# Two-block transformer kernel: the second layer's slabs in another order, the last up slab in narrow matmuls, and moved steps on four engines

## The chip, the cores and the metric

The kernel runs on one core of a Trainium2 chip. The metric is the device time of one execution in microseconds (us), lower is better. Engines: TensorE (PE) multiplies, ScalarE (ACT), VectorE (DVE) and GpSimd (POOL) do the rest, SyncE (SP) issues the loads. They run side by side and wait for each other on semaphores; each works through its own queue in order.

## What is computed

Two blocks, one after the other, on 256 tokens of width 1024, all in float32. The first is a mixer (8 heads of softmax attention, 4 heads of gated linear attention) and an FFN with a three-tap convolution over the tokens; then a norm with a gain; the second is a mixer of four branches and an FFN. Cut to what matters here:

```python
# first block, after its mixer
hn = rms_norm(x, ffn_norm_g[l])
h = causal_dwconv(hn @ w_ffn_up[l], conv_w[l], conv_b[l])     # 3 taps + bias
h_gate, h_val = h[..., :D_FF], h[..., D_FF:]                  # D_FF = 2816
x = x + (jax.nn.silu(h_gate) * h_val) @ w_ffn_down[l]
...
return rms_norm(x, final_norm_g)
# second block, mixer
proj = xn @ w_in
(cb, cc, cx, uv, sb_q, sb_k, sb_v, fx_q, fx_k, fx_v, f_raw, gate_raw) = split(proj)
y_a = cb * conv(cc * cx)                         # short convolution
y_b = u * (tril(w_s) @ layer_norm(v) + b_s)      # u, v = gelu(uv): spatial gate
y_c = stick_breaking_attention(sb_q, sb_k, sb_v)             # 4 heads of 64
log_f = log_sigmoid(f_raw + b_f)
y_d = forgetting_attention(rms(fx_q), rms(fx_k), fx_v, cumsum(log_f))   # 4 heads of 64
merged = sum over n of sigmoid(gate_n) * (y_n @ w_branch_n)
h = h + merged @ w_out
```

## The kernel before

**Slabs.** All weights are cut into 117 slabs of 1 MB (`STREAM`), each [128, 8, 256] for a projection of 256 columns. `AT` gives a slab's number n. A slab is loaded by SyncE into `raw` (3 buffers), rounded by ScalarE to a high part `hiw` (`rnd`, L611), and VectorE forms the rest `low = raw - hiw` (`res`, L1054), 3 buffers each. Activations are kept as a high and a low part as well (`xhi`, `xlo`; `yhi`, `ylo`), and a product is three matmuls: high by high, low by high, high by low (`three`, L1709 to L1711). `rnd(n)` waits until TensorE has used slab n-3 (`consumed`), `res(n)` for `rnd(n)`, and TensorE for `hi_made` and `lo_made` of its slab.

**Orders.** The order of the work is written out by hand on each engine: PE, ACT and DVE each have a loop over k, the slab's place in the stage (`for k, name in enumerate(IN2 + EARLY)` on PE, `for k in range(19)` on the others), in which `if k == ...` places the small steps of attention and convolution. A step that waits holds everything behind it on its engine.

**PSUM** has 8 banks of [128, 512]. `tenant(name, bank)` lists who uses a bank in which order; `take_bank` waits until the tenant before has given it back, `frees` gives it back.

**End of the first mixer.** `out_1(c)` runs the four slabs of the output projection in the order o0, o2, o3, o1; each is four quarters of six matmuls (`out_slab`, `out_quarter`). Between them TensorE turns the probabilities of heads 6 and 7 (`turn_probs`, L1894) and multiplies them with the values (`moba_values(3)`, called in slab o3 after its first quarter). ScalarE makes the high part of the two gated pairs (`gla_hi`, L757), VectorE the low part (`gla_lo`, L1273).

**First FFN.** For each of 11 steps f: slabs g_f and v_f (up), d_f (down). An up slab is `feature_major_wide` (L1733, L1741): 16 matmuls of 512 columns take `xhi` and `xlo` side by side and leave two partial sums, and 16 of 256 add the low part of the weights. VectorE adds the two sums (`hidden_sum`, L1324) into SBUF, ScalarE applies the last tap and the bias (`tap2s`, L858), VectorE the other two taps (`conv`, L1342), ScalarE the silu of the gate half, VectorE the product (`gate_1`, L1354), ScalarE its high part (`y_high`, L875), VectorE its low part (`y_low`, L1369). `last_two` writes out steps 9 and 10. TensorE ends with `ffn_down_last_two`: tile 0 (tokens 0 to 127) of d9 and d10, then tile 1.

**The norm between the blocks** (`weighted_norm` on DVE). As soon as a quarter is done, VectorE adds it to `h` (`quarter`, L1085), ScalarE squares it, VectorE sums the squares with weights (`weighted_sum`, L1108), GpSimd takes the root (L539), and the rows are scaled, one half by VectorE (`rows`, L1115), one by ScalarE (L652). TensorE turns a tile by 8 transposes (`turn_tile`, L1666), ScalarE writes `xhi` (`tile_turned`, L661), VectorE `xlo` (L1125).

**Second layer.** `IN2` is sq, sk, sv, fq, fk, fv, cc, cx, cb, u, v. The first slab (sq) is computed tile by tile, token-major (`tile_slab`, L1681, L1682, L1689), written out by ScalarE (`rows_out`, L668) and turned back by four transposes (`turn_back`, L1698) inside sv. sk uses `feature_major_late` (L1764, L1769), the others `project`. Steps in between: `stick_scores` (L2058, L2060), `stick_sums` (L2068), `fox_norm`, the product for the forget gates (`small_product("f")`), `fox_scores`, `turn_probs`.

## Time and profile before

| | us |
|---|---|
| median of 3 runs | 734.34 |
| runs | 734.33 to 734.43 |
| profiled execution | 734.29 |
| its span, first to last instruction | 732.5 |
| TensorE busy | 719.8 |
| VectorE busy | 546.8 |
| ScalarE busy | 379.8 |
| GpSimd busy | 56.9 |

The difference of 1.8 us between execution and span is what lies around the instructions. Stages on the trace's clock: first mixer to 131, first FFN to 321, second mixer to 543, second FFN to the end. A row of the timeline gives start, duration, engine, line, operation, names and shapes, count, and in brackets the idle time before it with what ended it. Matmuls are pipelined, so the duration of one is longer than the distance to the next start.

### The profile page before, as it was taken

The page shows a single profiled execution, that of the slowest core. Times are in us where ns is not written, and L with a number is a line of the kernel's source. Part 1 is how long each engine was busy: PE and PEld are TensorE (multiplying, and loading weights), DVE is VectorE, ACT ScalarE, POOL GpSimd, SP SyncE. Part 2 cuts the span into 40 slices and gives each one's busy share as a digit, 9 for nine tenths or more (in the row PEclk, how much of TensorE's full clock was granted, in tenths as well). Part 3 has the DMA queues.
Part 4 walks back from the last instruction along what each step waited for, and adds up shares of the span by engine and source line. Part 5 has one row for each costly group of instructions (what it writes and reads, how often), then busy time and mean ns, then how long its engine had stood idle before and what let it go on. Part 6 is the DMA issues. An engine that isn't in the chain of part 4 may idle for free.

```text
span 732.5 us, 11499 instructions
## 1 busy us (share of the span) xinstructions
PE 719.8 (98%) x4488; PEld 637.4 (87%) x4488; DVE 546.8 (75%) x645; ACT 379.8 (52%) x471; POOL 56.9 (8%) x62
## 2 busy tenths in 40 slices
PE   8999999999999999989999999999999999999998
PEld 8999987888888888778999888989888888888886
DVE  6679937889998889966557858787788666656673
ACT  7635466666455455556564544544456344343341
POOL 1455100000330000011000000000000000000000
PEclk9999999999999999999999999999999999999999
DMA  9846334255555455324543444445435554455431
GB/s 363 319 134 201 117 115 162 81 218 222 180 205 196 172 190 212 119 111 154 197 163 129 164 173 173 173 173 222 180 115 201 205 200 198 172 199 202 174 115 57
DMA packets 18954, 129.27 MB, mean 176 GB/s; under 512 B 2272, under 2 KB 2528, under 8 KB 3680
## 3 DMA queue, kind: packets, MB, share of 16 engines
q1 hardware_dynamic: 18912, 128.68, 47.4%
q8 instruction: 30, 0.49, 0.3%
q14 instruction: 12, 0.10, 0.0%
HBM read 126.57 MB, written 1.05 MB: 174 GB/s over the span
## 4 chain that ended last, share of the span: by engine, by line
PE 92%; DVE 3%; ACT 2%; issue 1%; DMA 1%; POOL 0%; SPq 0%; DVEq 0%; ACTq 0%
PE ps L1733 20%; PE ps L1709 14%; PE ps L1710 13%; PE ps L1711 13%; PE ps L1741 10%; PE ps L1753 8%; PE ps L1755 4%; DVE low L1054 1%; PE ps L1871 1%; ACT hiw L611 1%; PE ps L1681 1%; PE ps L1689 1%; PE ps L1682 1%; PE ps L1666 1%; DMA h<-in_x 1%
## 5 line engine op out<-in xcount | busy, mean ns | idle before, releaser
L611 ACT ACTIVATE hiw<-raw 128x2048 fp32r<-128x2048 f32 x116 | 222.0, 1915 | 203.6 <-PE ps L1741 97.7
L1054 DVE TENSOR_TENSOR low<-raw,hiw 128x2048 fp32r<-128x2048 f32 x116 | 267.2, 2308 | 79.4 <-ACT hiw L611 78.7
L1733 PE MATMUL ps<-xx,hiw 128*128 128x512 f32 x672 | 159.9, 390 | 0.0
L1733 PEld LDWEIGHTS ps<-xx,hiw 128*128 128x128 f32 x672 | 124.5, 188 | 24.8
L1741 PEld LDWEIGHTS ps<-xx,low 128*128 128x128 f32 x672 | 86.0, 191 | 3.1
L1741 PE MATMUL ps<-xx,low 128*128 128x256 f32 x672 | 87.3, 283 | 0.0
L1709 PE MATMUL ps<-hiw,yhi 128*128 128x512 f32 x208 | 81.8, 393 | 1.6 <-DVE ylo L1369 1.5
L1710 PE MATMUL ps<-low,yhi 128*128 128x512 f32 x208 | 81.2, 390 | 0.0
L1711 PE MATMUL ps<-hiw,ylo 128*128 128x512 f32 x208 | 80.9, 389 | 0.0
L1324 DVE TENSOR_REDUCE arena<-ps 128x512 f32<-128x1024 f32 x42 | 51.3, 1221 | 24.1 <-PE ps L1741 24.0
L1709 PE MATMUL ps<-xx,hiw 128*128 128x256 f32 x224 | 64.3, 287 | 1.0 <-DVE low L1054 1.0
L1753 PE MATMUL ps<-xx,hiw 128*128 128x512 f32 x256 | 64.7, 394 | 0.0
L1710 PE MATMUL ps<-xx,hiw 128*128 128x256 f32 x224 | 63.4, 283 | 0.0
L1711 PE MATMUL ps<-xx,low 128*128 128x256 f32 x224 | 63.3, 283 | 0.0
L1753 PEld LDWEIGHTS ps<-xx,hiw 128*128 128x128 f32 x256 | 46.1, 189 | 8.9 <-issue 0.5
L1709 PEld LDWEIGHTS ps<-hiw,yhi 128*128 128x128 f32 x208 | 39.1, 188 | 10.1 <-DVE ylo L1369 1.9
L1711 PEld LDWEIGHTS ps<-hiw,ylo 128*128 128x128 f32 x208 | 39.0, 188 | 8.3
L1710 PEld LDWEIGHTS ps<-low,yhi 128*128 128x128 f32 x208 | 39.1, 188 | 7.2
L1342 DVE SCALAR_TENSOR_TENSOR arena<-arena,vec 128x255 f32<-128x255 f32 x88 | 40.5, 481 | 5.8 <-ACT arena L858 1.5
L1709 PEld LDWEIGHTS ps<-xx,hiw 128*128 128x128 f32 x224 | 42.9, 192 | 2.0 <-issue 1.7
L1710 PEld LDWEIGHTS ps<-xx,hiw 128*128 128x128 f32 x224 | 42.9, 192 | 0.0
L1711 PEld LDWEIGHTS ps<-xx,low 128*128 128x128 f32 x224 | 42.9, 192 | 0.0
(240 smaller groups left out, 1022.2 us busy)
## 6 DMA issues: line engine op xcount, KB each, us to landing
raw<-in_slabs SPq DMA_DIRECT2D x117, 1024.0 KB, 4.8
vec<-in_vec SPq DMA_DIRECT2D x1, 1258.5 KB, 9.2
cst<-in_cst SPq DMA_DIRECT2D x1, 1220.0 KB, 12.8
h<-in_x SPq DMA_DIRECT2D x2, 512.0 KB, 3.6
arena<-arena SPq DMA_DIRECT2D x16, 64.0 KB, 2.9
out<-h SPq DMA_DIRECT2D x1, 512.0 KB, 2.7
out<-h SPq DMA_DIRECT2D x2, 256.0 KB, 2.0
vec<-in_vec SPq DMA_DIRECT2D x1, 229.0 KB, 4.3
```

What stands on the lines that cost most here:

```text
L611: act.activation(hiw[:, n % SPLIT, :], raw[:, n % RAW, :], ACT.Copy).then_inc(hi_made, 1)
L1054: dve.tensor_tensor(low[:, n % SPLIT, :], raw[:, n % RAW, :], hiw[:, n % SPLIT, :].bitcast(F32), ALU.subtract).then_inc(lo_made, 1)
L1324: dve.tensor_reduce((hid if k == "ffn1" else up)[par][j], wide_hidden(j).rearrange("p c (a b) -> p c b a", a=2), AX_X, ALU.add).then_inc(h ...
L1342: ins = dve.scalar_tensor_tensor(out=dst[:, o:], in0=src[:, 0:T - o], scalar=w, in1=dst[:, o:], op0=ALU.mult, op1=ALU.add)
L1666: mm = pe.transpose(bank(name)[:, k * P:(k + 1) * P], hn[n][:, tt, kt * P:(kt + 1) * P], ident)
L1709: pe.matmul(o, whi, mhi, start=start, stop=False)
L1710: pe.matmul(o, whi, mlo, start=False, stop=False)
L1711: return pe.matmul(o, wlo, mhi, start=False, stop=stop)
L1733: pe.matmul(banks[:, c, :], hi[:, kt, cc_], xx[:, kt].rearrange("p a b -> p (a b)"), start=kt == 0, stop=False)
L1741: mm = pe.matmul(banks[:, c, 0:T], lo[:, kt, cc_], xhi[:, kt, :], start=False, stop=kt == KT - 1)
L1753: pe.matmul(o, hi[:, kt, cc_], xx[:, kt].rearrange("p a b -> p (a b)"), start=kt == 0, stop=False)
L1755: mm = pe.matmul(o[:, 0:T], lo[:, kt, cc_], xhi[:, kt, :], start=False, stop=kt == KT - 1)
```

## The change

1. **Second layer.** `IN2` becomes v, sv, sq, sk, fq, fk, fv, cc, cx, cb, u. The first two are computed by the new `value_tile`, tile by tile and in parts ("both" = xhi by high and low weights, "high", "low", "second" = xlo by high weights), and stay token-major. `tile_slab`, `rows_out` and `turn_back` are no longer used there. Banks are dealt out anew, and the steps placed by k move: stick attention two slabs later, fox attention one, convolution one, the layer norm and the spatial gate one. The product for the forget gates goes from k = 7 to k = 3, its bias to k = 4, its exponential and logarithm to k = 6 and the forget sums from k = 8 to k = 7.
2. **Last up slab** (v10 of the first FFN): 48 matmuls of 256 columns into two banks (`last_up`) in place of the wide form; ScalarE (`last_tap2s`) and VectorE (`last_conv`) read PSUM directly, and `hidden_sum` falls away for it.
3. **Norm between the blocks.** VectorE scales both halves of tile 0's rows (`late_rows`), ahead of the third quarter. Tile 1's weighted sums stand after all low halves of tile 0, ScalarE rounds sv ahead of tile 0's high halves, and VectorE takes sv's residual (`res(second)`) ahead of tile 1's low halves.
4. **End of the first mixer.** Head 7 is turned inside slab o3, after its first quarter, its values follow after the second. The high part of the first gated pair is a copy on VectorE.

```diff
-IN2 = ["sq", "sk", "sv", "fq", "fk", "fv", "cc", "cx", "cb", "u", "v"]
+IN2 = ["v", "sv", "sq", "sk", "fq", "fk", "fv", "cc", "cx", "cb", "u"]
...
+        for n, b in (("v", 0), ("sv", 1), ("sq", 2), ("sk", 3), ("fq", 6), ("fk", 7), ("fv", 0), ("cc", 1), ("cx", 0),
+                     ("cb", 1), ("u", 0)):
...
+        tenant("f", 4)
...
-            for j in range(2):
-                gla_hi(j)
+            gla_hi(1)
...
+            def last_tap2s():
+
+                act.wait_ge(*hidden_full("ffn1", FF - 1, 1))
+                for c in range(2):
+                    ch = NCH // 2 + 2 * (FF - 1) + c
+                    act.activation(yb[0][:, 2 + c, :], last_hidden(c), ACT.Identity,
+                                   scale=V("cw")[:, 2 * NCH + ch:2 * NCH + ch + 1],
+                                   bias=V("cb")[:, ch:ch + 1]).then_inc(s("tap2"), 1)
...
                 tap2s(g, 0)
                 rnd(before[2][0])
                 silu_1(g)
+                last_tap2s()
                 rnd(after[2][0])
-                tap2s(g, 1)
                 y_high("ffn1", g)
                 rnd(after[3][0])
...
             for nh in range(2):
                 square(2, 0, nh)
-            rows(2, 0)
-            square(2, 1, 0)
+            rnd(b2 + 1)
             tile_turned(2, 0)
-            square(2, 1, 1)
-            rnd(b2 + 1)
+            for nh in range(2):
+                square(2, 1, nh)
             rows(2, 1)
             tile_turned(2, 1)
-            for tt in range(TT):
-                rows_out(2, 0, tt)
             rnd(b2 + 2)
...
-                if k == 7:
+                    forget_gates()
+                if k in (7, 9):
...
+            def late_rows(n, tt):
+
+                dve.wait_ge(s("root_made"), 2 * (n - 1) + tt + 1)
+                dve.tensor_scalar(hn[n][:, tt, D // 2:], h[:, tt, D // 2:], norm_scale(n, tt), None,
+                                  ALU.mult).then_inc(s("rows_b"), 1)
...
-            def weighted_norm(used):
+            def weighted_norm(used, second):
 
                 quarter(2, 0, used)
                 quarter(2, 1, used)
                 for nh in range(2):
                     weighted_sum(0, nh)
+                rows(2, 0)
+                late_rows(2, 0)
                 quarter(2, 2, used)
-                rows(2, 0)
-                weighted_sum(1, 0)
                 tile_turned(2, 0, range(0, 4))
                 quarter(2, 3, used)
-                tile_turned(2, 0, range(4, 6))
-                weighted_sum(1, 1)
-                tile_turned(2, 0, range(6, 8))
+                tile_turned(2, 0, range(4, 8))
+                for nh in range(2):
+                    weighted_sum(1, nh)
                 rows(2, 1)
+                res(second)
                 tile_turned(2, 1, range(8))
...
-            gla_norm(0)
-            gla_scaled(1)
+            for j in range(2):
+                gla_scaled(j)
+            gla_gated(0)
+            dve.wait_ge(s("gy_made"), 1)
+            dve.tensor_copy(yhi[:, 4:6, :], orr[0]).then_inc(s("gy_hi"), 1)
             gla_lo(0)
             gla_gated(1)
...
+            def last_conv():
+
+                f = FF - 1
+                for c in range(2):
+                    ch = NCH // 2 + 2 * f + c
+                    dve.wait_ge(s("tap2"), 4 * f + 2 + c + 1)
+                    dst, src = yb[0][:, 2 + c, :], last_hidden(c)
+                    for tap in (1, 0):
+                        o = 2 - tap
+                        ins = dve.scalar_tensor_tensor(out=dst[:, o:], in0=src[:, 0:T - o],
+                                                       scalar=V("cw")[:, tap * NCH + ch:tap * NCH + ch + 1],
+                                                       in1=dst[:, o:], op0=ALU.mult, op1=ALU.add)
+                        if tap:
+                            me.step(dve, ins)
+                        else:
+                            ins.then_inc(s("conv_made"), 1)
...
                 y_low("ffn1", f)
                 conv(g, 0)
                 split_all(before[2])
-                hidden_sum("ffn1", g, 1)
-                conv(g, 1)
+                last_conv()
...
-                if k == 6:
+                if k == 8:
                     for j in range(2):
                         fox_normed(j)
-                if 2 <= k <= 5:
-                    stick_soft(k - 2)
-                if k in (5, 7):
-                    head_lo(f"so{(k - 5) // 2}", 4 + (k - 5) // 2)
-                if k == 8:
+                if 4 <= k <= 7:
+                    stick_soft(k - 4)
+                if k in (7, 9):
+                    head_lo(f"so{(k - 7) // 2}", 4 + (k - 7) // 2)
+                if k == 7:
+                    forget_sums()
+                if k == 9:
...
                         mm = pe.matmul(o[:, 0:T], lo[:, kt, cc_], xhi[:, kt, :], start=False, stop=kt == KT - 1)
                     mm.then_inc(*fills(f"{name}_{c}"))
 
+            def value_tile(name, tt, parts, last=True):
+
+                n = AT[("in2", name)]
+                hi, lo = slab_views(n, KT)
+                t_ = slice(tt * P, (tt + 1) * P)
+                o = bank(name)[:, tt * 256:(tt + 1) * 256]
+                mm = None
+                for part in parts:
+                    if part == "high":
+                        pe.wait_ge(hi_made, n + 1)
+                    elif part in ("both", "low"):
+                        pe.wait_ge(lo_made, n + 1)
+                    for kt in range(KT):
+                        stop = last and part == parts[-1] and kt == KT - 1
+                        if part in ("high", "both"):
+                            if kt % 2 == 0:
+                                pe.wait_ge(s("xhi_made"), KT + 16 + 8 * tt + kt + 2)
+                            mm = pe.matmul(o, xhi[:, kt, t_], hi[:, kt, :], start=kt == 0, stop=False)
+                        if part in ("low", "both"):
+                            mm = pe.matmul(o, xhi[:, kt, t_], lo[:, kt, :], start=False, stop=stop)
+                        if part == "second":
+                            if kt % 2 == 0:
+                                turned, k = turned_at(2, tt, kt)
+                                pe.wait_ge(*part_given(turned, k + 2))
+                            mm = pe.matmul(o, xlo[:, kt, t_], hi[:, kt, :], start=False, stop=stop)
+                return mm
+
             def feature_major_late(o, n):
...
-                    if q == 1 and middle is not None:
-                        middle()
+                    if q in (1, 2) and middle is not None:
+                        middle[q - 1]()
                     mm = out_quarter(n, q, chunks, yh, yl, accs[q], first, last)
...
-            turn_probs(7, "mt7", pex1)
-            out_1(2, lambda: moba_values(3))
+            out_1(2, (lambda: turn_probs(7, "mt7", pex1), lambda: moba_values(3)))
             out_1(3)
...
+            def last_up():
+
+                n = AT[("ffn1", f"v{FF - 1}")]
+                pe.wait_ge(*hidden_free("ffn1", FF - 1, 1, done=False))
+                pe.wait_ge(lo_made, n + 1)
+                hi, lo = slab_views(n, KT)
+                for c in range(2):
+                    cc_ = slice(c * P, (c + 1) * P)
+                    for kt in range(KT):
+                        mm = three(last_hidden(c), hi[:, kt, cc_], lo[:, kt, cc_], xhi[:, kt, :], xlo[:, kt, :], kt == 0,
+                                   kt == KT - 1)
+                mm.then_inc(hidden_full("ffn1", FF - 1, 1)[0], 1)
...
-                ffn_up(k, FF - 1)
+                if k == "ffn1":
+                    ffn_up(k, FF - 1, parts=1)
+                    last_up()
+                else:
+                    ffn_up(k, FF - 1)
...
             for k, name in enumerate(IN2 + EARLY):
-                how = token_major if name in ("sv", "fv", "v") else feature_major
+                how = token_major if name == "fv" else feature_major
                 if k == 0:
-                    tile_slab(2, 0, 0)
+                    take_bank(pe, "v")
+                    value_tile("v", 0, ("both", "second"))
+                    take_bank(pe, "sv")
+                    value_tile("sv", 0, ("high", "second"), False)
                     turn_tile(2, 1)
-                    tile_slab(2, 0, 1)
+                    value_tile("v", 1, ("both",), False)
+                    value_tile("sv", 0, ("low",))
+                    value_tile("v", 1, ("second",)).then_inc(*fills("v"))
                 elif k == 1:
-                    take_bank(pe, name)
-                    pe.wait_ge(hi_made, AT[("in2", name)] + 1)
-                    feature_major_late(bank(name), AT[("in2", name)]).then_inc(*fills(name))
-                elif k == 2:
-                    def back():
-                        take_bank(pe, "sq")
-                        turn_back(2, 0, bank("sq")).then_inc(*fills("sq"))
-
-                    project("in2", name, lambda o, n: token_major(o, n, back))
+                    value_tile("sv", 1, ("both", "second")).then_inc(*fills("sv"))
                 elif name in EARLY:
                     gate_slab("in2", name)
                 else:
                     project("in2", name, how)
...
+                if k == 3:
+                    small_product("f", slice(16, 144))
+                if k == 8:
                     for j in range(2):
                         fox_norm(j)
```

**TensorE, from the turning of tile 0 to the turning of tile 1.** `tile_slab` for sq is L1681, L1682 (products) and L1689; in the change `value_tile` is L1812 (high weights), L1814 (low weights) and L1819 (xlo). Before:

```order
L1711 MATMUL ps<-hiw,ylo 128x512
L1666 MATMUL ps<-cst,arena 128x128 x8
L1709 MATMUL ps<-hiw,yhi 128x512
L1710 MATMUL ps<-low,yhi 128x512
...
L1711 MATMUL ps<-hiw,ylo 128x512
L1681 MATMUL ps<-hiw,xx 128x256
L1682 MATMUL ps<-low,xx 128x256
...
L1689 MATMUL ps<-hiw,xx 128x256 x8
L1666 MATMUL ps<-cst,arena 128x128 x8
```

Now:

```order
L1748 MATMUL ps<-hiw,ylo 128x512
L1703 MATMUL ps<-cst,arena 128x128 x8
L1746 MATMUL ps<-hiw,yhi 128x512
L1747 MATMUL ps<-low,yhi 128x512
...
L1748 MATMUL ps<-hiw,ylo 128x512
L1812 MATMUL ps<-hiw,xx 128x256
L1814 MATMUL ps<-low,xx 128x256
...
L1819 MATMUL ps<-hiw,xx 128x256 x8
L1812 MATMUL ps<-hiw,xx 128x256 x8
L1819 MATMUL ps<-hiw,xx 128x256 x8
L1703 MATMUL ps<-cst,arena 128x128 x8
```

Between the two turnings (L1666, now L1703) stood the last quarter and one tile of sq; now the last quarter, tile 0 of v, and 16 matmuls of tile 0 of sv stand there.

**VectorE, from the last up slab to the turning of tile 0.** L1324 is the sum of the partials, L1342 and L1377 the taps, L1054 and L1067 residuals, L1085 and L1098 the additions to `h`, L1115, L1128 and L1134 the scaled rows. Before:

```order
L1054 TENSOR_TENSOR low<-raw,hiw 128x2048
L1324 TENSOR_REDUCE arena<-ps 128x512
L1342 SCALAR_TENSOR_TENSOR arena<-arena,vec 128x255
...
L1354 TENSOR_TENSOR arena<-arena 128x512
L1054 TENSOR_TENSOR low<-raw,hiw 128x2048
L1369 TENSOR_TENSOR ylo<-arena,yhi 128x512
L1054 TENSOR_TENSOR low<-raw,hiw 128x2048
L1085 TENSOR_TENSOR h<-ps,h 128x512 x2
L1108 ISA arena,st<-arena 128x512
...
L1085 TENSOR_TENSOR h<-ps,h 128x512
L1115 TENSOR_SCALAR arena<-h,st 128x512
```

Now:

```order
L1067 TENSOR_TENSOR low<-raw,hiw 128x2048
L1377 SCALAR_TENSOR_TENSOR arena<-ps,vec,arena 128x255
L1377 SCALAR_TENSOR_TENSOR arena<-ps,vec,arena 128x254
...
L1391 TENSOR_TENSOR arena<-arena 128x512
L1067 TENSOR_TENSOR low<-raw,hiw 128x2048
L1406 TENSOR_TENSOR ylo<-arena,yhi 128x512
L1067 TENSOR_TENSOR low<-raw,hiw 128x2048
L1098 TENSOR_TENSOR h<-ps,h 128x512 x2
...
L1128 TENSOR_SCALAR arena<-h,st 128x512
L1134 TENSOR_SCALAR arena<-h,st 128x512
L1098 TENSOR_TENSOR h<-ps,h 128x512
```

The sum is gone, the taps read PSUM, and the rows come in two halves ahead of the third quarter's addition.

**VectorE, at the forget sums.** L1484 to L1490 (now L1520 to L1526) are the forget sums, L1469 (now L1504) the stick argument, L1478 (now L1513) the fox query and key. Before, at k = 8:

```order
L1501 SCALAR_TENSOR_TENSOR arena<-arena,vec 128x255
L1501 SCALAR_TENSOR_TENSOR arena<-arena,vec 128x254
L1565 TENSOR_TENSOR arena<-ps,arena 128x512
L1484 SCALAR_TENSOR_TENSOR arena<-arena 128x256
L1486 SCALAR_TENSOR_TENSOR arena<-arena 128x256
L1490 TENSOR_SCALAR arena<-arena 2x2x256 x4
L1054 TENSOR_TENSOR low<-raw,hiw 128x2048
L1444 TENSOR_TENSOR ylo<-arena,yhi 128x512
```

Now, at k = 7 and 8:

```order
L1067 TENSOR_TENSOR low<-raw,hiw 128x2048
L1498 SCALAR_TENSOR_TENSOR arena<-arena 128x384
L1269 TENSOR_TENSOR ylo<-ps,yhi 128x256
L1520 SCALAR_TENSOR_TENSOR arena<-arena 128x256
L1522 SCALAR_TENSOR_TENSOR arena<-arena 128x256
L1526 TENSOR_SCALAR arena<-arena 2x2x256 x4
L1504 TENSOR_TENSOR arena<-arena,ps 128x384
L1597 TENSOR_TENSOR arena<-ps,arena 128x512
L1067 TENSOR_TENSOR low<-raw,hiw 128x2048
L1513 SCALAR_TENSOR_TENSOR arena<-ps,vec,arena 64x2x256 x4
L1537 SCALAR_TENSOR_TENSOR arena<-arena,vec 128x255
```

They stood behind the product with cb, ahead of a residual; now they stand between head 0's low part and the last stick argument.

## Rows read from the trace of the kernel before

**Rows 1.** Page, part 1: engine, busy us (share of the span), instructions
```profile
PE 719.8 (98%) x4488; PEld 637.4 (87%) x4488; DVE 546.8 (75%) x645; ACT 379.8 (52%) x471; POOL 56.9 (8%) x62
```
**Rows 2.** Waits of TensorE: engine, line, waited for: us in total, times, longest
```profile
PE ps L1709 <- DVE ylo L1369: 1.5, 1, 1.5
```
**Rows 3.** Windows (us from the span's start): length, busy us per engine
```profile
core 0: us, PE busy (x) PEld busy (x) DVE busy (x) ACT busy (x) POOL busy (x), PEclk, DMA share, GB/s
...
301.50:331.00 29.50, 25.35 (x140) 21.09 (x140) 22.97 (x41) 17.09 (x35) 3.13 (x8) 1.00 0.29 107
331.00:345.00 14.00, 12.79 (x108) 12.42 (x106) 8.12 (x7) 7.58 (x8) 2.02 (x2) 1.00 0.41 150
345.00:397.00 52.00, 52.00 (x411) 48.73 (x410) 34.01 (x44) 29.92 (x42) 0.00 (x0) 1.00 0.45 163
```
**Rows 4.** Timeline of TensorE, slab o2's end and head 7
```profile
118.20 0.39 PE L1711 MATMUL ps<-hiw,ylo 128*128 128x512 f32 x1
119.20 0.52 PE L1894 MATMUL ps<-cst,arena 128*128 128x128 f32 x3 [0.61 <-DVE arena L1241]
```
**Rows 5.** Timeline of TensorE, slab v10 to the turning of tile 0
```profile
295.28 3.82 PE L1733 MATMUL ps<-xx,hiw 128*128 128x512 f32 x16
298.94 2.08 PE L1741 MATMUL ps<-xx,low 128*128 128x256 f32 x16
300.85 0.40 PE L1709 MATMUL ps<-hiw,yhi 128*128 128x512 f32 x1
...
308.81 0.39 PE L1711 MATMUL ps<-hiw,ylo 128*128 128x512 f32 x1
310.68 0.49 PE L1709 MATMUL ps<-hiw,yhi 128*128 128x512 f32 x1 [1.49 <-DVE ylo L1369]
...
317.40 0.39 PE L1711 MATMUL ps<-hiw,ylo 128*128 128x512 f32 x1
319.06 1.06 PE L1666 MATMUL ps<-cst,arena 128*128 128x128 f32 x8 [1.27 <-DVE arena L1115]
```
**Rows 6.** Timeline of VectorE, same stretch
```profile
303.16 1.22 DVE L1324 TENSOR_REDUCE arena<-ps 128x512 f32<-128x1024 f32 x1
305.11 1.91 DVE L1342 SCALAR_TENSOR_TENSOR arena<-arena,vec 128x255 f32<-128x255 f32 x4 [0.74 <-ACT arena L858]
...
307.74 2.29 DVE L1054 TENSOR_TENSOR low<-raw,hiw 128x2048 fp32r<-128x2048 f32 x1
309.94 0.69 DVE L1369 TENSOR_TENSOR ylo<-arena,yhi 128x512 fp32r<-128x512 f32 x1
...
317.83 0.69 DVE L1085 TENSOR_TENSOR h<-ps,h 128x512 f32<-128x512 f32 x1 [1.73 <-PE ps L1711]
318.44 0.48 DVE L1115 TENSOR_SCALAR arena<-h,st 128x512 f32<-128x512 f32 x1
```
**Rows 7.** Timeline of GpSimd, the root of tile 0
```profile
316.19 0.56 POOL L539 TENSOR_TENSOR st<-st 128x1 f32<-128x1 f32 x1 [96.77 <-DVE st L1108]
```
**Rows 8.** Timeline of TensorE, the start of the second layer
```profile
324.49 0.50 PE L1689 MATMUL ps<-hiw,xx 128*128 128x256 f32 x2 [0.34 <-DVE xx L1125]
325.21 1.06 PE L1666 MATMUL ps<-cst,arena 128*128 128x128 f32 x8 [0.22 <-DVE arena L1115]
...
330.27 4.10 PE L1764 MATMUL ps<-xx,hiw 128*128 128x256 f32 x32 [0.47 <-ACT arena L668]
...
339.08 0.60 PE L1698 MATMUL ps<-cst,arena 128*128 128x128 f32 x4
...
342.75 0.70 PE L2058 MATMUL ps<-arena 64*128 64x256 f32 x4 [0.20 <-ACT arena L675]
...
344.69 0.36 PE L1709 MATMUL ps<-xx,hiw 128*128 128x256 f32 x1 [1.01 <-DVE low L1054]
```
**Rows 9.** Timelines of VectorE and TensorE, forget sums to the first fox turning
```profile
392.37 1.71 DVE L1490 TENSOR_SCALAR arena<-arena 2x512 f32<-2x512 f32 x4
...
401.31 0.35 DVE L1241 TENSOR_SCALAR arena<-arena,st 128x256 f32<-128x256 f32 x1
...
403.13 0.49 PE L1894 MATMUL ps<-cst,arena 128*128 128x128 f32 x3
```

132 lines of the change are left out of this document (64 added, 68 removed).

## Prediction, on record before the changed kernel ran

> **What bounds the kernel now.** I read the page first. TensorE is busy for 719.8 of 732.5 us [rows 1]. A kernel like that can only gain where TensorE starts late, or where it has an instruction less to issue. The list of what TensorE waited for is short, no entry is over 1.5 us, and one of the two longest is the low part of the gated values [rows 2]. The windows say where. Between 301.5 and 331 us TensorE is idle for 29.50 - 25.35 = 4.2 us, between 331 and 345 for 1.2 us, and between 345 and 397 for nothing, all at a granted clock of 1.00 [rows 3]. That 301 to 345 is the end of the first FFN and the start of the second layer, where this change works. From 345 us to the last norm nothing waits, so what is gained before moves the rest forward whole, if no new wait appears.
>
> A busy TensorE row covers the drain of a matmul, so I count from start to start. 16 matmuls of 256 columns take 300.85 - 298.94 = 1.91 us, 0.119 each; 16 of 512 columns take 298.94 - 295.28 - 0.01 = 3.65 us, 0.228 each [rows 5]. A start later than the one before it plus its pace is lost time.
>
> **Last heads of the first layer.** The turning of head 7 starts at 119.20; the matmul before it started at 118.20 and ends its issue at 118.43, so 0.77 us is lost [rows 4]. The change issues six matmuls (1.37 us) in between. The reciprocal and scaling that it waits for then ends about 0.5 us ahead. The value product of heads 6 and 7 moves behind a second quarter, and the copy of the turned probabilities, a rounding and the low part of these heads follow it on ScalarE and VectorE; by the same spacings they end at about 125.1, and the fourth slab would start at 125.0. So about 0.1 comes back. The high half of the first gated pair goes from ScalarE to VectorE; it is at best 0.2 us sooner, since the hop over ScalarE's table load goes away. Bounds: 0 (the new wait takes all) to 1.0. I take **0.7**, near the row of the wait that goes.
>
> **The last up slab, made narrow.** Removed: 16 matmuls of 512 and 16 of 256 columns, 5.57 us (295.28 to 300.85); added 48 of 256, 48 x 0.119 = 5.73. **Cost 0.17 us** [rows 5]. By the Trainium skill (VectorE: DVE Perf Modes, the section on the TRN2 errata) a matmul takes 6 cycles plus its columns at 2.4 GHz: 48 x 0.109 against 16 x 0.216 + 16 x 0.109, so the form would cost 0.04 us and the sum would be 0.13 better; the trace's own pace disagrees and decides. For this TensorE stops writing the two partial sums that VectorE must add. The sum (L1324) is 1.22 us long and starts at 303.16, because a residual stands ahead of it; four taps follow (1.91), then the gate (0.69), a residual (2.29, next start 2.20 later), and the low part until 309.94 + 0.69 = 310.63 [rows 6]. TensorE, done issuing at 309.04, starts at 310.68: 1.64 lost [rows 5]. Now ScalarE makes its tap straight from PSUM while VectorE is still in that residual, and VectorE begins the four taps at 303.16: taps to 305.1, gate to 305.9, residual to 308.1, low part to 308.7. TensorE asks at 309.04 + 0.17 = 309.21. All 1.64 goes, with 0.5 to spare. The taps read PSUM now and no row has that form with 255 elements; they are costed from the SBUF taps, 0.48 each, with the 512-element PSUM addition (0.69, first row at L1085) as upper end: at 0.69 each the low part would be 0.9 later and 0.4 of the gain would be lost. The Trainium skill (same page and section) prices a VectorE read from PSUM 62 cycles above one from SBUF, which speaks against the move: 4 x 0.065 = 0.26 us, still inside the 0.5. **Gain 1.64.**
>
> **Turning of the first tile.** It starts at 319.06; TensorE was free at 317.40 + 0.23 = 317.63, so 1.43 is lost [rows 5]. It waits for the scaled rows (L1115) at 318.44. These had their root from GpSimd at 316.19 + 0.56 = 316.75, but VectorE stood in the third quarter's addition (L1085 at 317.83), which itself had waited 1.73 for TensorE [rows 6, 7]. Now both row halves stand ahead of it on VectorE. The chain from quarter 1 to the root is unchanged and shifts with TensorE: root at about 315.2, rows 315.7 and 316.1. TensorE is ready at 316.1. I leave 0.1: **gain 1.33**.
>
> **Start of the second layer.** Lost there now [rows 8]: 0.50 for the low half of tile 0's last columns (324.49), 0.38 ahead of the second turning (325.21), 0.63 ahead of sk (330.27), which also waits for rows that sq leaves, 0.36 for the four transposes that turn sq back (339.08), 0.35 ahead of the stick scores (342.75) and 1.18 ahead of fq (344.69), whose low part had hung on a rounding that waited for sq's late evacuation. The change puts v and sv first, both token-major, so nothing is turned back and no slab hangs on that evacuation; 24 + 16 matmuls of 256 columns lie between the turnings (4.8 us after the last quarter, before 2.9). From the spacings: xlo of tile 0 is complete at about 320.3 and its last pair is asked for at 321.0; root of tile 1 at 322.4, rows at 322.9 (VectorE) and 323.1 (ScalarE), TensorE ready at 323.2. The wait behind the second turning remains, since the first products still need xhi from ScalarE (1.43 from turning to product, as now). The residual of sv, put ahead of tile 1's low halves, ends at 325.1 and is asked for at 326.7; the low halves end at 327.1 and are asked for from 327.7. sq's residual ends at 330.2, asked for at 331.5. So 0.50, 0.28, 0, 0.63, 0.36, 0.35 and 1.18 go: **3.3 us**. Bounds: 0.9 less, if the second turning waits as long as before and the low halves bind, and 0.6 more.
>
> **Forget sums sooner, everything one or two slabs later.** TensorE's work here is the same instructions in another order. On VectorE the forget sums (about 2.9 us, of which the four narrow copies are 1.71 [rows 9]) leave the place ahead of slab b2+11's residual and stand behind head 0's low part, ahead of the fourth stick argument. I walked both from sq's start at 0. TensorE: a slab of 48 matmuls is 5.8 us with its switch, the forget product 24 x 0.119 = 2.9, and the small attention products between slabs 0.7 to 0.9 each (fox norms 1.7). So cx ends at 49.2, the sums of head 3 at 51.7, u at 64.3, the first gate slab at 70.5, and the turning of fox head 0 is asked for at 71.2. VectorE: residual b2+10 to 48.8, soft part and low part of head 0 to 49.5, forget sums to 52.4, while head 3's sums are ready at 51.9: 0.5 late. Then stick argument and gate product to 53.6; ScalarE's exponential and rounding (0.5 + 1.9) to 55.3; residual to 57.6; fox query and key (3.1) to 60.7, asked for at 64.3; taps and cb product to 63.4, with which bank 1 is free, asked for at 64.9; residual and two low parts to 66.5; mask and maximum (1.3) to 67.8; residual to 70.0; scaling to 70.7. The tightest margin is the last, 0.4; before, the scaling ended at 401.66 and the turning came at 403.13, 1.5 us of margin [rows 9]. **Cost 0**; without that cover up to 1.5.
>
> **The sum.** 0.7 + 1.64 - 0.17 + 1.33 + 3.3 = 6.8 us. The profiled execution took 734.29 us (span 732.5), 0.05 under the median 734.34. 734.34 - 6.8 = **727.5 us**, 0.93% less. A measurement of this kernel can tell 0.2% (1.5 us) from no change.
>
> **Rivals.**
> - *VectorE crowded between the forget sums and the first fox turning.* For it: margins of 0.4 and 1.5 us, and VectorE works in order. Against: it is busy only 34.0 of 52 us there [rows 3]. It costs 0.7 to 2: 728.2 to 729.5 us. Chance 0.18.
> - *The norm binds in another place.* Both tiles' squares and sums now stand behind more of VectorE's and ScalarE's queue (a rounding of sv ahead of tile 0's high halves, which waits for TensorE to finish the slab before). If the second turning and the high halves wait, 1 to 2.5 us stay: 728.5 to 730. Chance 0.15.
> - *No gain at all:* waits only change names, since each was hiding another one right behind it. It would take over 5 us of new waits in 40 us; 733 to 735.5. Chance 0.02.
> - *Slower:* the low parts of the second layer's slabs come after their slab's turn. VectorE then sets the pace from fq to u (7 slabs), since each residual stands behind stick, fox and forget work that waits for TensorE. It decides from 1.0 us per slab, 7 us in all; at 1.4 the time is 737.3. Against: a residual now lands over 5 us ahead of its slab, and TensorE waits for none from 345 us on [rows 3]. Chance 0.02.
>
> My forecast has 0.63. **Range 726.4 to 730.8**: its low end takes the favourable bounds of the norm and heads (another 1.0), its high end both first rivals in part. Faster by over 0.2% 0.96, within 0.2% 0.02, slower 0.02.
>
> **What would show it.** Right: no TensorE wait on L1369's successor at the last down slab; turning of tile 0 within 0.3 us of the matmul before; no 1 us wait ahead of fq; TensorE again without idle from there to the last norm. The span from the last up slab's start to the start of the fox scores of head 0 (295.28 to 396.08, 100.8 us) holds one more slab after the change: 100.8 - 6.1 + 5.8 = 100.5 us. Wrong: a wait of over 0.5 us at the first fox turning, at bank 1 after u, or at the second turning; or a fourth out slab that starts over 0.5 us after its predecessor.

## The result, and the profile after

The changed kernel takes **727.08 us** (median of 4 runs, 726.98 to 727.10), the kernel before in the same job 734.35 (4 runs, 734.33 to 734.43). The ratio is 0.9897, with a 95% interval of 0.9885 to 0.9909: 7.27 us less. 727.5 had been forecast, in a range of 726.4 to 730.8.

The profiled execution has a span of 725.3 us. The page's first part and the list of TensorE's waits, which answer to [rows 1] and [rows 2]:

```profile
PE 717.6 (99%) x4500; PEld 637.4 (88%) x4500; DVE 547.6 (76%) x646; ACT 377.6 (52%) x467; POOL 60.0 (8%) x62
```
```profile
PE ps L1746 <- DVE xx L1088: 1.3, 1, 1.3
PE ps L1691 <- DVE arena L1080: 1.2, 1, 1.2
PE ps L1678 <- POOL zeros L559: 1.0, 1, 1.0
PE ps L1812 <- ACT xx L663: 0.4, 1, 0.4
PE ps L1718 <- ACT xx L663: 0.3, 2, 0.2
```

Five entries are left. The first three lie in the first 11 us, the fourth is the one wait left in the norm ahead of the second layer, and the last is two waits of 0.2 us at most in the other norms. The wait for the low part of the gated values is gone. The windows, which answer to [rows 3]:

```profile
core 0: us, PE busy (x) PEld busy (x) DVE busy (x) ACT busy (x) POOL busy (x), PEclk, DMA share, GB/s
...
301.50:331.00 29.50, 29.13 (x183) 26.19 (x182) 25.84 (x43) 19.52 (x35) 6.89 (x10) 1.00 0.42 145
331.00:345.00 14.00, 14.00 (x119) 14.00 (x118) 9.41 (x7) 7.19 (x6) 1.37 (x1) 1.00 0.71 275
```

TensorE's idle time between 301.5 and 331 us fell from 4.15 to 0.37 us, that between 331 and 345 from 1.2 to nothing. The timeline of TensorE at the four places of the prediction, which answers to [rows 4, 5, 8]: head 7's turning, the last down slab's start and the first turning of the norm, the second turning's products.

```profile
119.87 0.49 PE L1958 MATMUL ps<-cst,arena 128*128 128x128 f32 x3
120.12 0.48 PE L1746 MATMUL ps<-hiw,yhi 128*128 128x512 f32 x1
...
300.51 0.40 PE L1746 MATMUL ps<-hiw,yhi 128*128 128x512 f32 x1
...
308.47 0.39 PE L1748 MATMUL ps<-hiw,ylo 128*128 128x512 f32 x1
308.69 0.39 PE L1746 MATMUL ps<-hiw,yhi 128*128 128x512 f32 x1
...
315.27 0.39 PE L1748 MATMUL ps<-hiw,ylo 128*128 128x512 f32 x1
315.50 1.04 PE L1703 MATMUL ps<-cst,arena 128*128 128x128 f32 x8
...
323.96 0.36 PE L1812 MATMUL ps<-hiw,xx 128*128 128x256 f32 x1 [0.37 <-ACT xx L663]
```

315.27 to 315.50 is one matmul's pace: the turning of tile 0 starts without any loss. So does the last down slab at 308.69. Only 323.96 has a wait. VectorE around both, which answers to [rows 6], with GpSimd's root, which answers to [rows 7], behind it:

```profile
302.62 1.90 DVE L1377 SCALAR_TENSOR_TENSOR arena<-ps,vec,arena 128x255 f32<-128x255 f32 x4
304.63 0.69 DVE L1391 TENSOR_TENSOR arena<-arena 128x512 f32<-128x512 f32 x1
305.24 2.29 DVE L1067 TENSOR_TENSOR low<-raw,hiw 128x2048 fp32r<-128x2048 f32 x1
307.44 0.69 DVE L1406 TENSOR_TENSOR ylo<-arena,yhi 128x512 fp32r<-128x512 f32 x1
...
314.73 0.49 DVE L1128 TENSOR_SCALAR arena<-h,st 128x512 f32<-128x512 f32 x1 [0.68 <-POOL st L541]
315.13 0.48 DVE L1134 TENSOR_SCALAR arena<-h,st 128x512 f32<-128x512 f32 x1
315.70 0.69 DVE L1098 TENSOR_TENSOR h<-ps,h 128x512 f32<-128x512 f32 x1
```
```profile
314.14 0.56 POOL L541 TENSOR_TENSOR st<-st 128x1 f32<-128x1 f32 x1 [95.26 <-DVE st L1121]
```

The low part ends at 308.13, 0.56 us ahead of its use at 308.69 (0.5 was forecast).

**Where the 7.27 us came from.** The stretch from the last up slab to fox head 0's scores, which now holds one slab of 5.8 more, is 394.68 - 294.75 = 99.9 us against 100.8. That is a gain of 6.7 us (6.1 was forecast). The last heads of the first layer gave 0.8 (0.7 was forecast). The first product with the normed activations (`ps<-xx,smh`) started 0.27 us later in this execution (10.05, before 9.79). That is no effect of the change: the parts x1 to x4 have it at 9.91 to 10.01 and y8 at 9.81, with the same start of the program. 6.7 + 0.8 - 0.3 = 7.2.

### The profile page after: what moved, and what is told of

It reads as the page before. It is cut to its first block, busy times and chain, and to the rows that moved or that the text cites. A ratio compares the mean times of both kernels' runs of the same rounds, so it can differ in the third digit from the quotient of the medians.

```text
span 725.3 us, 11521 instructions
## 1 busy us (share of the span) xinstructions
PE 717.6 (99%) x4500; PEld 637.4 (88%) x4500; DVE 547.6 (76%) x646; ACT 377.6 (52%) x467; POOL 60.0 (8%) x62
## 4 chain that ended last, share of the span: by engine, by line
PE 98%; DMA 1%; ACT 0%; DVE 0%; issue 0%; SPq 0%
PE ps L1770 21%; PE ps L1746 15%; PE ps L1747 15%; PE ps L1748 15%; PE ps L1778 11%; PE ps L1790 8%; PE ps L1792 4%; PE ps L1935 1%; PE ps L1958 1%; PE ps L1965 1%; PE ps L1718 1%; DMA h<-in_x 1%; PE ps L1703 1%; PE ps L1812 1%; PE ps L1819 1%; PE ps L1726 1%
## 5 line engine op out<-in xcount | busy, mean ns | idle before, releaser
L1067 DVE TENSOR_TENSOR low<-raw,hiw 128x2048 fp32r<-128x2048 f32 x116 | 267.0, 2306 | 78.7 <-ACT hiw L613 78.1
L1770 PE MATMUL ps<-xx,hiw 128*128 128x512 f32 x656 | 156.1, 390 | 0.0
L1770 PEld LDWEIGHTS ps<-xx,hiw 128*128 128x128 f32 x656 | 121.6, 188 | 24.1
L1778 PEld LDWEIGHTS ps<-xx,low 128*128 128x128 f32 x656 | 84.0, 191 | 3.0
L1778 PE MATMUL ps<-xx,low 128*128 128x256 f32 x656 | 85.2, 283 | 0.0
L1746 PE MATMUL ps<-xx,hiw 128*128 128x256 f32 x272 | 78.1, 287 | 0.0
L1747 PE MATMUL ps<-xx,hiw 128*128 128x256 f32 x272 | 77.0, 283 | 0.0
L1748 PE MATMUL ps<-xx,low 128*128 128x256 f32 x272 | 77.0, 283 | 0.0
L1790 PE MATMUL ps<-xx,hiw 128*128 128x512 f32 x256 | 64.9, 395 | 0.0
L1790 PEld LDWEIGHTS ps<-xx,hiw 128*128 128x128 f32 x256 | 46.2, 189 | 9.0 <-issue 0.5
L1746 PEld LDWEIGHTS ps<-xx,hiw 128*128 128x128 f32 x272 | 52.2, 192 | 1.2 <-issue 0.7
L1747 PEld LDWEIGHTS ps<-xx,hiw 128*128 128x128 f32 x272 | 52.2, 192 | 0.0
L1748 PEld LDWEIGHTS ps<-xx,low 128*128 128x128 f32 x272 | 52.2, 192 | 0.0
L1361 DVE SCALAR_TENSOR_TENSOR arena<-arena,vec 128x255 f32<-128x255 f32 x84 | 38.6, 480 | 5.0 <-ACT arena L859 0.7
```

The source lines that it names most:

```text
L1067: dve.tensor_tensor(low[:, n % SPLIT, :], raw[:, n % RAW, :], hiw[:, n % SPLIT, :].bitcast(F32), ALU.subtract).then_inc(lo_made, 1)
L1361: ins = dve.scalar_tensor_tensor(out=dst[:, o:], in0=src[:, 0:T - o], scalar=w, in1=dst[:, o:], op0=ALU.mult, op1=ALU.add)
L1746: pe.matmul(o, whi, mhi, start=start, stop=False)
L1747: pe.matmul(o, whi, mlo, start=False, stop=False)
L1748: return pe.matmul(o, wlo, mhi, start=False, stop=stop)
L1770: pe.matmul(banks[:, c, :], hi[:, kt, cc_], xx[:, kt].rearrange("p a b -> p (a b)"), start=kt == 0, stop=False)
```

## The experiments

Twelve kernels ran. Each compares with the kernel before on the same chip (734.45 in the first job of four, 734.47 to 734.49 in the others). The changed kernel's 727.08 is of another job, whose kernel before took 734.35, so a difference from 727.08 is uncertain by some 0.1 us.

### One part alone: do the waits add?

**x1_up_only**: the kernel before with the narrow last up slab, ScalarE's taps from PSUM and VectorE's taps on them, and no partial sums.

```diff
-                hidden_sum("ffn1", g, 1)
-                conv(g, 1)
+                last_conv()
```


> The kernel before with the narrow last up slab alone. If each removed wait of TensorE passes whole to the end of the kernel (additive theory): the 1.64 us ahead of the last down slab go, 0.17 us of more matmuls come, so the time is 734.35 - 1.47 = 732.9 us, with no wait of TensorE for the low part. Rival (waits hide one another: VectorE, which has to finish the same residuals and taps, hands the time to the next wait behind it, at the norm): a gain under 0.5 us, 733.9 or more, and the wait for the scaled rows of tile 0 longer than its 1.43 us. Second rival (taps that read PSUM are dearer, 0.69 us each or more): about 0.4 us of wait left, 733.3.

Measured: 732.85 us (732.79 to 733.76), ratio 0.9979 (0.9970 to 0.9988): 1.60 less. The slab cost and the turning behind, in TensorE's timeline:

```profile
295.47 0.28 PE L1742 MATMUL ps<-xx,hiw 128*128 128x256 f32 x1
...
301.23 0.40 PE L1742 MATMUL ps<-hiw,yhi 128*128 128x512 f32 x1
```
```profile
317.65 0.52 PE L1699 MATMUL ps<-cst,arena 128*128 128x128 f32 x3 [1.27 <-DVE arena L1131]
```

The slab takes 5.76 us, 0.19 more than the 5.57 of before. The turning still waits 1.27, as before, so the wait behind it absorbed nothing. The additive theory holds, with a little more than the 1.47 expected; the section on the prediction says why.

**x2_heads_only**: the kernel before with the order of the last heads and the copy of the first gated pair by VectorE.

```diff
-            turn_probs(7, "mt7", pex1)
-            out_1(2, lambda: moba_values(3))
+            out_1(2, (lambda: turn_probs(7, "mt7", pex1), lambda: moba_values(3)))
```


> The kernel before with the change at the first layer's last heads alone (head 7 turned behind the first quarter of the fourth out slab, the first gated pair's high half copied by VectorE). Additive theory: the time between the heads and the first norm shortens as in the changed kernel's own trace, 0.8 us: 733.5 us. Rival (the fourth slab's start waits anew for the low part, so that the stall only moves): within 0.2 us of 734.35.

Measured: 733.63 us (733.51 to 735.71), ratio 0.9990 (0.9981 to 1.0000): 0.82 less, as expected by the first theory. The interval touches 1, but the lowest run (733.51) lies 0.80 under the lowest of before (734.31), and the trace shows the same 0.83 between the first product with activations and the first turning of the first norm. (The slab within which head 7 is turned is o3, the third in order; the expectation calls it the fourth.)

**x3_rows_only**: the kernel before with VectorE scaling both halves of tile 0's rows ahead of the third quarter's addition, and ScalarE none of them. Of the diff, VectorE's part:

```diff
-                quarter(2, 2, used)
                 rows(2, 0)
+                late_rows(2, 0)
+                quarter(2, 2, used)
```


> The kernel before with one edit: both halves of tile 0's scaled rows are made by VectorE ahead of the third quarter's addition, ScalarE makes none of them. Theory (the 1.43 us ahead of the turning of tile 0 were VectorE standing in that addition): the turning follows the slab within 0.1 us. How much of it stays depends on the order behind, which is unchanged here: if the chain to the second turning and to the low half (0.50 and 0.38 us of waits) is tied to the end of the down slab and not to the first turning, these waits grow and only part passes: 0.5 to 1.0 us gain, 733.4 to 733.9. If each wait passes whole: 733.0. Rival (the third quarter is now later by two scalings, 1.0 us, and so is the root of tile 1; TensorE gets back at the second turning all it gained at the first): within 0.2 us of 734.35.

Measured: 734.28 us (733.88 to 736.48), ratio 1.0000 (0.9991 to 1.0009), so unclear by the runs. The profiled run took 733.88, and four others 733.89 to 734.03. Its trace shows what happened:

```profile
317.49 0.40 PE L1717 MATMUL ps<-hiw,ylo 128*128 128x512 f32 x1
317.73 1.04 PE L1672 MATMUL ps<-cst,arena 128*128 128x128 f32 x8
```
```profile
324.09 0.50 PE L1695 MATMUL ps<-hiw,xx 128*128 128x256 f32 x2 [1.14 <-DVE xx L1130]
```
```profile
322.75 0.75 DVE L1107 CUSTOM_DVE_ANT_0 arena<-arena,st 128x512 f32<-128x512 f32 x1 [0.38 <-ACT arena L646]
...
323.43 0.60 DVE L1130 SCALAR_TENSOR_TENSOR xx<-ps,vec,xx 128x128 fp32r<-128x128 f32 x2
```

The 1.43 us ahead of the first turning are gone. Of them 0.8 come back at the low half of tile 0's last columns, whose loss grew from 0.50 to 1.30, and 0.16 in small steps ahead of it: VectorE makes that low half behind the sum of tile 1 (L1107), and that chain did not become shorter. Behind it TensorE is 0.5 us ahead of the kernel before, and stays so. **The one edit alone is worth 0.5 us by the trace, in the new order 1.5** (y2 below). The changed kernel has both more of TensorE's work between the turnings and tile 1's sums behind all low halves of tile 0; no run tells which of the two lets the gain through. Only here did a removed wait pass into the next.

**x4_order_and_norm**: the changed kernel without the parts of x1 and x2, so the new order of slabs, norm and forget sums alone.

> The changed kernel without the narrow last up slab and without the heads' change: the new order of slabs, of the norm and of the forget sums alone. If the parts are additive, it is 727.08 + 1.47 + 0.82 = 729.4 us, 5.0 us under the kernel before. If the new order needs VectorE free earlier, as the narrow up slab makes it (the last residuals and the norm's sums then stand in its way), it is over 730.0. If the narrow up slab's gain would have been absorbed by other waits anyway, it is under 729.0.

Measured: 729.55 us (729.37 to 730.38), ratio 0.9939 (0.9925 to 0.9953): 4.90 less. 1.60 + 0.82 + 4.90 = 7.32, and the whole change gives 7.27. By the medians the parts add, and the trace shows the two waits of the parts left out (1.48 at the last down slab, 0.6 at head 7) as they were.

### One part undone

**y1_forget_back**:

```diff
                     dve.tensor_tensor(yv, two("cb"), yv, ALU.mult).then_inc(*frees("cb"))
+                    forget_sums()
...
-                if k == 7:
-                    forget_sums()
```


> The changed kernel with the forget sums of VectorE put back behind the gate product cb, ahead of the residual that follows it. Theory (the sums have to stand sooner only because the order of slabs now asks for VectorE's scaling of fox head 0 with 0.4 us of margin): 2.9 us more of VectorE's work stand between the taps and that scaling, so the first fox scores or the first turning wait 2 to 2.5 us and the time is about 729.3 us. Rival (VectorE has enough idle time behind cb to take them, since it is busy for only two thirds of that stretch): within 0.3 us of 727.1.

Measured: 729.11 us (729.05 to 731.35), ratio 0.9935 (0.9922 to 0.9949): 2.0 more than the changed kernel. TensorE waits twice, for the sums themselves and for the scaling of head 0:

```profile
396.24 0.46 PE L2162 MATMUL ps<-arena 128*128 128x128 f32 x2 [1.54 <-DVE arena L1526]
...
403.55 0.52 PE L1957 MATMUL ps<-cst,arena 128*128 128x128 f32 x3 [0.18 <-DVE arena L1261]
```

So the move keeps 2.0 us that the new order of slabs would lose. No run has it in the old order, where the margin was 1.5 us [rows 9] and nothing waited.

**y2_rows_back**: tile 0's rows as in the kernel before. Of the diff, VectorE's part (ScalarE scales the second half again):

```diff
-                rows(2, 0)
-                late_rows(2, 0)
                 quarter(2, 2, used)
+                rows(2, 0)
```


> The changed kernel with tile 0's scaled rows as before: VectorE's half behind the third quarter's addition, the other half on ScalarE. Theory: the turning of tile 0 waits 1.3 to 1.5 us again, and since nothing behind it waits in the new order, all of that reaches the end: 728.4 to 728.6 us. Rival (as the third quarter's addition then comes sooner, the second tile's root comes sooner too and a later wait shrinks): under 0.5 us, below 727.6.

Measured: 728.58 us (728.50 to 730.12), ratio 0.9922 (0.9908 to 0.9936): 1.50 more. The turning waits as before, and nothing behind it gives any of it back.

```profile
318.41 0.41 PE L1703 MATMUL ps<-cst,arena 128*128 128x128 f32 x2 [1.27 <-DVE arena L1129]
```

**y3_residual_late**: VectorE takes the residual of sv behind tile 1's low halves.

```diff
-                res(second)
                 tile_turned(2, 1, range(8))
+                res(second)
```


> The changed kernel with the residual of the second slab (sv) behind tile 1's low halves on VectorE. Theory (prediction's margins: the residual ended 1.6 us ahead of its use, the low halves of tile 1 0.6 us ahead): the residual then ends about 1.4 us later than it is asked for, or 0.8 at best, and TensorE waits 0.5 to 1.5 us there: 727.6 to 728.6 us. Rival (the low halves, 2.0 us sooner, free something that TensorE waited for, or the order has room): within 0.3 us of 727.1.

Measured: 731.32 us, ratio 0.9947 (0.9933 to 0.9960), in two groups: 729.89 and 729.95, and 731.32, 731.44 and 731.56. Both theories missed, and so did my size. VectorE begins the low halves at 324.24, after 2.13 us without work, since ScalarE makes the high ones no sooner: the order saves nothing on them (324.36 in the changed kernel), and the residual, which had filled that time, comes on top. It ends at 328.6, and TensorE asked for it at 325.9. The lower group is the wait alone, 727.08 + 2.78. The upper has 1.5 us more. TensorE's rows in its profile (of the 731.32), and the windows around them:

```profile
328.66 0.58 PE L1814 MATMUL ps<-low,xx 128*128 128x256 f32 x1 [2.62 <-DVE low L1067]
...
330.53 1.72 PE L1819 MATMUL ps<-hiw,xx 128*128 128x256 f32 x8
332.08 0.28 PE L1812 MATMUL ps<-hiw,xx 128*128 128x256 f32 x1
```
```profile
core 0: us, PE busy (x) PEld busy (x) DVE busy (x) ACT busy (x) POOL busy (x), PEclk, DMA share, GB/s
...
326.00:328.00 2.00, 0.03 (x1) 0.00 (x0) 2.00 (x3) 1.98 (x2) 0.00 (x0) 1.00 0.00 0
328.00:330.00 2.00, 1.34 (x6) 1.35 (x7) 2.00 (x2) 0.34 (x1) 0.00 (x0) 0.61 0.27 33
330.00:331.00 1.00, 1.00 (x7) 1.00 (x7) 1.00 (x2) 0.00 (x0) 0.00 (x0) 0.50 0.48 180
331.00:332.00 1.00, 1.00 (x7) 1.00 (x7) 1.00 (x2) 0.00 (x0) 0.00 (x0) 0.57 0.98 418
332.00:333.00 1.00, 1.00 (x11) 1.00 (x10) 1.00 (x2) 0.72 (x2) 0.05 (x1) 1.00 0.96 401
```

After an idle stretch of 2.6 us the granted clock is at 0.50, the 1.2 GHz level, for some 3 us. The 16 products from 328.66 to 332.08 take 3.42 us where 16 at 0.12 take 1.92: that is the 1.50. Only this run has a trace, but the mean granted clock of every run is on record. It is 0.998 in the three upper runs and 0.999 in the two lower ones.

**y4_gla_copy_back**: the first gated pair's high half by ScalarE again. Of the diff, VectorE's part:

```diff
-            for j in range(2):
-                gla_scaled(j)
-            gla_gated(0)
-            dve.wait_ge(s("gy_made"), 1)
-            dve.tensor_copy(yhi[:, 4:6, :], orr[0]).then_inc(s("gy_hi"), 1)
+            gla_norm(0)
+            gla_scaled(1)
```


> The changed kernel with the first gated pair's high half back on ScalarE. Prediction's theory (this part of the change was worth at most 0.2 us, the heads' turning the rest): 727.1 to 727.3 us. Rival (the copy on ScalarE is what made the fourth out slab's low part late): a new wait of TensorE at the fourth slab and 727.6 us or more.

Measured: 727.57 us (727.53 to 728.33), ratio 0.9904 (0.9889 to 0.9919): 0.49 more, so the copy is worth more than the 0.2 that I gave it, but not by the rival's mechanism. The profiled execution began 0.8 us late, so it is read from start to start:

```profile
113.92 0.50 PE L1748 MATMUL ps<-hiw,yhi 128*128 128x512 f32 x1
```

The second slab (o2) starts 0.22 us later behind the values of heads 4 and 5 (113.92 against a pace start of 113.70), since VectorE ends the pair's low part at 113.86. The third slab (o3) starts 0.1 us late behind its residual, with another 0.1 to its second product. Together that is 0.41 of the 0.49. No wait came up at the fourth slab.

### The clock behind a wait

**y7_late_filled**: y3 with TensorE kept busy while it would wait.

```diff
                     value_tile("v", 1, ("both",), False)
+                    for _ in range(20):
+                        pe.matmul(bank("sv")[:, 0:P], zeros[:, :], zeros[:, :], start=False, stop=False)
                     value_tile("sv", 0, ("low",))
```


> The changed kernel with the late residual of sv, as in y3_residual_late, and 20 products with zeros (0.1 us each, added to sv's sum, so its value stays) ahead of the products that wait for it. In y3_residual_late TensorE waited 2.78 us, and the time came out at 729.9 in two runs and at 731.4 in three; its profile shows a granted clock of 0.50 behind the wait. Theory (it is the idle engine whose clock falls, and the 1.5 us more are slower products behind the wait): filled, no run is at 731.4, the profile shows a clock of 1.00 there, and the time is 729.9 to 730.1 us. Rival (the clock falls for another reason, or products with zeros do not count): runs at about 731.4 again.

Measured: 731.60 us (731.50 to 734.18), ratio 0.9961 (0.9948 to 0.9975). The time is the rival's, but the cause is not. The clock stayed at 1.00 in every window from 12 us on, and the products with zeros took 4.39 us, 0.22 each and not 0.1. They overfill the wait by 1.6 us: 727.08 + 4.39 = 731.5. So the time alone could not decide. The clock on record speaks for the theory: 1.000 in each of the three runs from 731.50 to 731.60, where the upper runs of y3 have 0.998.

**y8_late_filled_short**: the same with `range(12)`.

> As y7_late_filled, with 12 products with zeros in place of 20. There each of the 20 took 0.22 us (4.39 us in all, where 2.78 were to be filled), TensorE waited for nothing, its granted clock stayed at 1.00, and the time was 731.5. Now they take 2.63 us and leave a wait of some 0.15. Theory (the 1.5 us on top in three of the five runs of y3_residual_late were the lower clock behind an idle stretch, and y7's time is only the length of its filling): the time is 727.08 + 2.8 to 2.9 = 729.9 to 730.0 us, with no run at 731.4 but for one whose span begins late, and the clock is 1.00 there. Rival (y7's 731.5 has the same cause as y3's, whatever the clock shows in one profile): about 731.4 again.

Measured: 729.97 us, and all five runs lie between 729.73 and 730.04; ratio 0.9936 (0.9922 to 0.9950). The window where y3 had 0.61:

```profile
328.00:330.00 2.00, 2.00 (x17) 1.86 (x17) 2.00 (x2) 0.18 (x1) 0.00 (x0) 1.00 0.12 16
```

The same residual is as late as in y3, and the work of the kernel is the same but for the 12 products. With TensorE busy, no run of five pays the 1.5 us that three of five paid when it idled, and their mean granted clock is 0.999 to 1.000.

### What GpSimd and VectorE do to each other

In the changed kernel GpSimd's two broadcast copies run beside VectorE's gate of the residual stream. GpSimd's row and VectorE's row of the changed kernel:

```profile
329.14 3.23 POOL L594 COPY arena<-cst 128x1024 f32<-128x1024 f32 x2 [3.16 <-ACT arena L677]
```
```profile
329.41 4.04 DVE L1474 SCALAR_TENSOR_TENSOR h<-h,st,vec 128x1024 f32<-128x1024 f32 x2
```

**y5_fill_later**: GpSimd's copies wait for the low part of a later slab.

```diff
-            pool.wait_ge(*given_back("v"))
+            pool.wait_ge(lo_made, AT[("in2", "v")] + 5)
```


> The changed kernel with GpSimd's two broadcast copies (L594, 3.23 us beside VectorE's gate, where they took 2.02 before) held back by some five slabs. Theory (the two engines slow each other while both work): VectorE's two gate operations (L1474) go from 4.04 us back to about 2.5 us and GpSimd's copies to about 2.0 us; the time stays within 0.2 us of 727.1, since TensorE waited for neither. Rival (the gate is dearer in the new place for a reason of its own, such as the root of the residual or where its data lie): L1474 stays at about 4 us.

Measured: 727.01 us (726.88 to 727.18), ratio 0.9896 (0.9881 to 0.9912), the same time as the changed kernel. Its rows of VectorE and of GpSimd:

```profile
329.31 2.48 DVE L1474 SCALAR_TENSOR_TENSOR h<-h,st,vec 128x1024 f32<-128x1024 f32 x2
```
```profile
336.46 2.02 POOL L594 COPY arena<-cst 128x1024 f32<-128x1024 f32 x2 [10.57 <-DVE low L1067]
```

Apart, they need 2.48 and 2.02 us, 4.50 in a row. Together they took from 329.14 to 333.45, 4.31 us: nearly one after the other, for no time of the kernel, since TensorE waits for neither. Of the two copies the first took 1.25 us and the second 2.04 (1.04 each in y5), and each gate operation some 2.06 (1.28 in y5).

### The wait that is left

**y6_norm_sooner**: tile 1's squares and sums are put inside tile 0's copies, and four products of sv's tile 0 behind the second turning. The values of v and sv are summed in another order. Of the diff, TensorE's part:

```diff
-                    value_tile("v", 0, ("both", "second"))
+                    value_tile("v", 0, ("both",), False)
                     take_bank(pe, "sv")
-                    value_tile("sv", 0, ("high", "second"), False)
+                    value_tile("sv", 0, ("high",), False)
+                    value_tile("v", 0, ("second",))
+                    value_tile("sv", 0, ("second",), False, range(0, 4))
                     turn_tile(2, 1)
+                    value_tile("sv", 0, ("second",), False, range(4, 8))
```


> The changed kernel, its last wait in the norm taken up: ScalarE's and VectorE's squares and sums of tile 1 stand inside the copies of tile 0, the second turning stands ahead of the last four of the second products of sv's tile 0, and these fill the time in which the high half of tile 1 is made. Theory: the 0.54 us between the second turning and the products behind it go and a wait for the rows of at most 0.1 comes: 726.6 to 726.8 us. Rival (the copies of tile 0, now later by a square or a sum each, hold up the second products, or the roots do not come sooner, since GpSimd's root waits for both sums): a new wait of 0.3 to 1 us, 727.0 to 727.7 us.

Measured: **726.66 us** (726.51 to 726.67), ratio 0.9892 (0.9877 to 0.9907), as the theory had it: 0.42 under the changed kernel, and 0.35 under y5, which ran in the same job with the changed kernel's time. The window that had 0.37 us of idle time is full:

```profile
301.50:331.00 29.50, 29.50 (x187) 26.70 (x187) 26.38 (x44) 20.00 (x36) 7.50 (x10) 1.00 0.44 147
```

## Why the prediction was right

**The bound** was right. TensorE set the time, the idle time between 301.5 and 345 us was there to be taken, and behind 345 us everything moved forward whole: the end of the second mixer's slabs and the end of the kernel both came 7.2 us sooner.

**Last heads** (0.7, measured 0.82, x2). The turning's loss of 0.77 goes, the fourth slab's start gives back 0.15 (125.14 to 125.40, and the next at 125.74), where 0.1 had been put. The copy gives 0.22 at the second slab's start, as forecast. y4 shows that it also prevents 0.19 us at the third slab's start, which the new place of head 7's turning would have cost and which I had not seen.

**Narrow up slab** (cost 0.17, measured 0.19, x1). The trace's own pace was the better price. The Trainium skill (VectorE: DVE Perf Modes, the section on the TRN2 errata) would have had 0.04, and the measurement decides against it. The gain of 1.64 came whole. The four taps from PSUM took 1.90 us against 1.91 from SBUF [rows 6], so neither my upper bound (0.69 each) nor the 62 cycles more per read from PSUM of the Trainium skill (same page and section) shows here.

**Turning of tile 0** (1.33, measured 1.43). The root was forecast at 315.2 and came at 314.70, the first half row ended at 315.22. In the whole these are on a clock that ran 0.5 us ahead of the forecast's, since the heads had gained. x3 shows what the prediction's sum did not say: this gain needs the rest of the new order, without which some 0.9 of it is lost again.

**Start of the second layer** (3.3, measured 3.7). It is the 6.7 of the stretch, less 1.43, less 1.64 and the 0.1 of its stop, plus 0.19. Each of the listed waits went, and the one behind the second turning stayed at 0.54, as forecast. The residual of sv ended 1.4 us ahead of its use (1.6 forecast), the low halves of tile 1 0.4 (0.6 forecast).

**Forget sums** (0, measured 0). The fourth stick argument came 0.5 late, as forecast, and the scaling of fox head 0 ended at 401.17 for a turning at 401.58: the margin is the 0.4 that had been walked out. VectorE's rows:

```profile
381.18 1.72 DVE L1526 TENSOR_SCALAR arena<-arena 2x512 f32<-2x512 f32 x4
382.92 0.55 DVE L1504 TENSOR_TENSOR arena<-arena,ps 128x384 f32<-128x384 f32 x1
...
400.82 0.35 DVE L1261 TENSOR_SCALAR arena<-arena,st 128x256 f32<-128x256 f32 x1
```

Without the move it costs 2.0 (y1), where "up to 1.5" had been put.

**The term that was mis-sized** is the 6.1 of the stretch from the last up slab on, which measured 6.7. 0.2 of it was my caution: 0.1 left at each of the two turnings, where nothing stayed of the one and only the wait behind it of the other. The rest is mostly what a stop costs. I counted a wait from the matmul before at its pace to the start behind it, and left out that the first matmul behind a stop is also slower to give way. TensorE of the kernel before, last down slab:

```profile
310.68 0.49 PE L1709 MATMUL ps<-hiw,yhi 128*128 128x512 f32 x1 [1.49 <-DVE ylo L1369]
311.02 0.39 PE L1710 MATMUL ps<-low,yhi 128*128 128x512 f32 x1
```

311.02 - 310.68 is 0.34 where the pace is 0.23, so a stop or a switch costs about 0.1 on top of its wait. Over the whole stretch, the 256- and 512-column matmuls that take 0.05 to 0.3 us beyond their pace (0.12 and 0.2275) to the next start add up to 3.2 us in 28 places before and to 2.9 us in 24 places after, although one more slab lies in it. So fewer stops gave 0.3 us. x1 shows one alone: it gave 1.60 and not 1.47. This is read from spacings; no run was made for it alone. Some 0.1 us of the 0.6 stays unexplained.

**The rivals.** None came: VectorE kept its margins, the norm bound nowhere else, no wait took another's place in the whole (in x3, a part alone, it did), and no residual was late. y3 shows how near the last was in kind: one residual behind the low halves costs 2.8 us, and in three of five runs 1.5 more.

## What to carry to other kernels

Where one engine is busy all the time, count its loss from start to start with its own pace, and expect some 0.1 us more for a stop that goes. A removed wait passes to the end only if the chain behind it is shortened or has room. So walk that chain too, since the same edit was worth 0.5 us in the old order and 1.5 in the new. A wait can cost more than itself when it lets TensorE's clock fall, as the 2.6 us of y3 did: if it can't be removed, fill it, and measure the filling.
